# One-hots built token by token as contiguous rows, with a third of the neighbouring weight splits on GpSimd

## The chip, the cores and the metric

The kernel runs on one core of a Trainium2 chip. The metric is the device time of one execution in microseconds (us). TensorE (PE) multiplies matrices, VectorE (DVE) and ScalarE (ACT) work elementwise, GpSimd (POOL) is a fourth elementwise engine, and SyncE (SP) starts most of the transfers between memory and the on-chip SBUF. Each engine works through its own instructions in order; semaphores order the engines against each other. Matmul results land in PSUM.

## The reference

Two transformer blocks in float32 over one sequence of 256 tokens, width 1024. The second one ends with a layer of product-key experts (PEER), and the change lies there. Cut to what matters:

```python
def block(xb):                                   # 128 tokens at a time
    q = (xb @ w_query).reshape(128, 8, 2, 128)
    s = jnp.einsum('thpc,pkc->thpk', q, sub_keys)
    s1, i1 = lax.top_k(s[:, :, 0], 16)
    s2, i2 = lax.top_k(s[:, :, 1], 16)
    cand = (s1[..., :, None] + s2[..., None, :]).reshape(128, 8, 256)
    sc, ci = lax.top_k(cand, 16)
    e = take(i1, ci // 16) * 128 + take(i2, ci % 16)     # which of 16384 experts
    g = jax.nn.softmax(sc, axis=-1)
    act = jax.nn.gelu(jnp.einsum('td,thkd->thk', xb, expert_u[e]))
    return jnp.einsum('thk,thkd->td', g * act, expert_v[e])
```

Each token chooses 8 x 16 = 128 of 16384 experts, with a weight g for each.

## The kernel before

The kernel gathers nothing. It multiplies all tokens with all of expert_u and expert_v and makes the choice by a weight that is zero for every expert that was not chosen. All weights of both blocks stream through SBUF as 421 units of 128 x 1024 float32 numbers: `load` (SP) fetches unit u into one of four raw slots, `split` on ScalarE writes its rounded high half whi (three slots), `split` on VectorE writes the low half wlo = raw - whi (three slots), and TensorE multiplies in three products, high with high, high with low, low with high. The units named in the table LO_POOL get their low half from GpSimd (`split` in pool_program, L2074) with a semaphore of its own, lo_pool; TensorE's `whole(u)` and SP's `load` wait for the one or the other.

Units EU to EU + 127 are expert_u: `cols` (L456) makes 24 matmuls of 256 columns for each, eight blocks times three products, and ScalarE's `take_u` puts gelu of the result through stage into memory. In the first half VectorE finds the chosen experts and their weights beside this (`route`, L1904). At unit TURN_AT = 65 these are turned so that a token is a column: i1T and i2T hold the first and second key index of the 128 choices of each of the 256 tokens, g_hi and g_lo its weight in two fp16 parts. From unit HOT_FROM = 66 on, `hot_groups` spreads 64 groups of four tokens over the remaining units. For group g:

- VectorE (`one_hots`, L1990) builds three fp16 tables for the four tokens in X's place, called room: the one-hot of the first key, and the one-hot of the second key times g_hi and times g_lo. It compares keys, which holds 0 to 127, with the indices, one whole group in an instruction; the token is the innermost axis of room. Two groups fit, so group g waits until group g - 2 was multiplied (weighed).
- TensorE (L916) multiplies, for each token, the one-hot of the first key with both others: two matmuls of 128 columns into a 128 x 128 table of weights, eight matmuls a group, after the matmuls of its unit.
- ScalarE (`take_weights`, L1331) copies the tables of a group out of PSUM.

VectorE's program for unit n is: the groups of n, then the low half of unit n + 2. ScalarE's is: the tables of unit n - 1, the high half of unit n + 2 (which needs unit n - 1 used up), gelu of unit n - 1.

Units EV to EV + 127 are expert_v: `accumulate` (L930) adds twelve matmuls of 512 columns per unit to four PSUM banks, (t, d) being the half of the tokens and of the width. The last three units are written apart from the loop (L946 to L955), so that the bank of t = 0, d = 0 is finished first, and the closing norm starts with it. The order of all work is written out by hand.

Of the kernel before, what the change touches and what calls it, by code (L numbers as in the profile page):

```python
# [9 lines left out]
F16 = mybir.dt.float16  # L10
I32 = mybir.dt.int32
U32 = mybir.dt.uint32
ALU = mybir.AluOpType
# [36 lines left out]
UNITS = 421  # L50
V_ORDER = [*range(120, 128), *range(120)]

LO_POOL = (BR_B + 1, BR_B + 2, BR_B + 3, OUT, OUT + 1, UP, UP + 1, IN2, IN2 + 1, QUERY, EV + 1)

EXP_AT, TURN_AT, HOT_FROM = 42, 65, 66

# [25 lines left out]
def build(nc, A, out):  # L82
    with ExitStack() as ctx:

        def sb(stack, name, shape, dt=F32):
            return stack.enter_context(nc.sbuf_tensor(name, shape, dt))

        def signal(name, events, step=1):
            return Signal(ctx.enter_context(nc.semaphore(f"s_{name}")), events, step)
# [45 lines left out]
        def cs(name):  # L135
            return cst[:, CST[name][0]:CST[name][1]]
# [110 lines left out]
        i2T = sb(p4, "i2T", [128, 256], F16)  # L247
        g_hi = sb(p4, "g_hi", [128, 256], F16)
        g_lo = sb(p4, "g_lo", [128, 256], F16)
        keys = sb(p4, "keys", [128, 128, 4], F16)  # L250
        stage = sb(p4, "stage", [128, 8, 256])
        room = X[:, :, :].rearrange("p t n -> p (t n)").bitcast(F16)[:, 0:3072].rearrange("p (s w k t) -> p s w k t", s=2, w=3, t=4)
        gb4, squares, fin = raw[:, 0, :], raw[:, 1, :], raw[:, 2:4, :]


# [164 lines left out]
        ln_d = signal("ln_d", ["mean", "vc", "v", "r", "gain0", "gain1", "vn", "mixed0", "mixed1", "gated1"])  # L420
        fold_d = signal("fold_d", ["00", "10", "01", "11"])
        last_d = signal("last_d", ["00", "10", "01", "11"])
        routed = signal("routed", range(1, 99))
        route_d = signal("route_d", ["ex", "done", "turned1", "turned2"])
        query_d = signal("query_d", [1, 3, 5, 7, 9, 11, 13, 15])
        score_d = signal("score_d", range(4))
        hot_key = signal("hot_key", range(64))
        hot = signal("hot", range(64))
        taken_v = signal("taken_v", range(128))
        cut_d = signal("cut_d", range(128))  # L430
# [5 lines left out]
        def tensor_program(e):  # L436
# [451 lines left out]
            for n in range(128):  # L888
                if n == 1:
                    score(3)  # L890
                whole(EU + n)
                b = 4 + n % 4
                if n in (0, 1):
                    e.wait_ge(*(score_a if n % 2 == 0 else score_d).at(2))
                elif n in (2, 3):
                    e.wait_ge(*(score_a if n % 2 == 0 else score_d).at(3))
                elif n >= 4:
                    e.wait_ge(*gelu_u.at(n - 4))
                m = cols(EU + n, 0, 8, TH, TL, ps[b][:, 0:256], range(4))
                if n == 127:  # L900
                    m.then_inc(*half_used("u"))
                cols(EU + n, 0, 8, TH, TL, ps[b][:, 0:256], range(4, 8)).then_inc(*used(EU + n))
                for g in hot_groups(n):
                    e.wait_ge(*hot.at(g))
                    if g < 4:
                        if g == 0:
                            e.wait_ge(*route_a.at("turned0"))
                        if g == 1:
                            e.wait_ge(*route_d.at("turned1"))
                        if g == 2:  # L910
                            e.wait_ge(*route_d.at("turned2"))
                    else:
                        e.wait_ge(*weight_a.at(g - 4))
                    for i in range(4):
                        for w in (1, 2):
                            m = e.matmul(ps[g % 4][:, i * 128:i * 128 + 128], room[:, g % 2, 0, :, i], room[:, g % 2, w, :, i],  # L916
                                         start=w == 1, stop=w == 2)
                    m.then_inc(*weighed(g))
                if n == TURN_AT:
                    e.wait_ge(*route_d.at("done"))  # L920
                    e.wait_ge(*query_d.at(15))
                    e.wait_ge(*query_a.at(14))
                    for i, src in enumerate((ii[0], ii[1], gg)):
                        for t in range(2):
                            m = e.transpose(ps[i][:, t * 128:t * 128 + 128], src[:, t * 128:t * 128 + 128], ident)
                        m.then_inc(*turned(f"route{i}"))
# [10 lines left out]
            for n in range(125):  # L937
# [5 lines left out]
                    for d in range(2):  # L943
                        m = accumulate(n, t, d)
                m.then_inc(*used(EV + n))
            for n in range(125, 128):  # L946
                whole(EV + n)
                e.wait_ge(*cut_d.at(n))
            for n, d in ((125, 0), (125, 1), (126, 0), (126, 1)):
                accumulate(n, 0, d)  # L950
            for t in range(2):
                for d in range(2):
                    for n in range(125 if t else 127, 128):
# [435 lines left out]
        def vector_program(e):  # L1389
# [483 lines left out]

            e.tensor_copy(keys[:, :, :], bc(cs("iota"), 2, 4))

            def best16(n, vals, idx, src):

# [108 lines left out]


            def one_hots(g):  # L1990
                s, ts = g % 2, slice(4 * g, 4 * g + 4)
                h1, h2, h2_low = (room[:, s, w, :, :] for w in range(3))
                if g >= 2:
                    e.wait_ge(*weighed.at(g - 2))
                e.tensor_tensor(h2_low, keys[:, :, :], bc(i2T[:, ts], 1, 128), ALU.is_equal).then_inc(*hot_key(g))
                e.tensor_tensor(h1, keys[:, :, :], bc(i1T[:, ts], 1, 128), ALU.is_equal)
                e.wait_ge(*hot_key.at(g))
                e.tensor_tensor(h2, h2_low, bc(g_hi[:, ts], 1, 128), ALU.mult)
                e.tensor_tensor(h2_low, h2_low, bc(g_lo[:, ts], 1, 128), ALU.mult).then_inc(*hot(g))  # L1999

            def take(i):
                v = V_ORDER[i]
# [13 lines left out]
            for n in range(128):  # L2016
                if n < 64:
                    pull(UB1)
                for g in hot_groups(n):
                    if g == 0:  # L2020
                        e.wait_ge(*route_a.at("g_hi"))
                        e.wait_ge(*route_d.at("turned2"))
                        e.wait_ge(*d_kept.at(0))
                    one_hots(g)
                if n == 1:
                    score(3)
                split(EU + n + 2)
                if n == 127:
                    take(0)
                    for i in range(3):  # L2030
                        take(i + 1)
                        cut(i)
                if n == TURN_AT:
                    e.wait_ge(*turned.at("route1"))
                    e.tensor_copy(i2T[:, :], ps[1][:, 0:256]).then_inc(*route_d("turned1"))
                    e.wait_ge(*turned.at("route2"))
                    e.wait_ge(*route_a.at("g_hi"))
                    e.scalar_tensor_tensor(out=g_lo[:, :], in0=ps[2][:, 0:256], scalar=G_SCALE, in1=g_hi[:, :],
                                           op0=ALU.mult, op1=ALU.subtract).then_inc(*route_d("turned2"))
# [32 lines left out]
        def pool_program(e):  # L2072
# [23 lines left out]
            split(QUERY)  # L2096
            e.wait_ge(*low.at("x4.7"))
            e.dma_start(sub[:, :, :], A["sub_keys_2"]).then_inc(*d_sub(0))
            split(EV + 1)
            e.wait_ge(*lo.at(UNITS - 1))  # L2100
            e.dma_start(gb4, A["final_norm_g_2"].partition_broadcast(128)).then_inc(*d_gb4(0))
# [170 lines left out]
```

## Time and profile before

| | |
|---|---|
| median of 3 runs | 1370.74 us (1369.51 to 1370.87) |
| profiled execution: time, span | 1368.58 us, 1366.8 us |
| TensorE matmuls, weight loads (share of the span) | 96%, 88% |
| VectorE, ScalarE, GpSimd | 69%, 51%, 2% |
| granted TensorE clock, mean | 0.991 |

The profile shows one execution; the busy shares are means over stages with different limits, so a stage has to be read by itself. Matmuls overlap each other, and the start of one to the start of the next is what one costs.

### The profile page before, as it was taken

To read this page: it belongs to the slowest core of one execution; us is meant where nothing else is said; L and a number is where in the kernel's file an instruction comes from. 1 tells how busy PE (TensorE), PEld (TensorE's weight loads), DVE (VectorE), ACT (ScalarE), POOL (GpSimd) and SP (SyncE) were. 2 spreads that over 40 slices of the span, in tenths; PEclk is the share of its full clock that TensorE was granted. 3 is DMA by queue.
4 is the path that set the end of the run, shared out by engine and by line. 5 is a ranking of instruction groups with operands and counts; after the bars stand their busy time and mean duration, and the time that the engine had idled before them with its cause. 6 is when DMAs were issued, how large, how long until landed. Compare 5 with 4: busy or idle time off the path is not lost.

```text
span 1366.8 us, 22018 instructions
## 1 busy us (share of the span) xinstructions
PE 1316.4 (96%) x8592; PEld 1200.9 (88%) x8592; DVE 943.5 (69%) x1792; ACT 690.4 (51%) x1135; POOL 33.1 (2%) x27
## 2 busy tenths in 40 slices
PE   7999998999989899999999999999999999999996
PEld 6889978998877678999999999999988888888885
DVE  5765676674456755999899666676667676767665
ACT  5566456664455744444454444444444545454553
POOL 0000130000020000000000000000000000000000
PEclk9999999999999998999999999999999999999999
DMA  7533455666646335477767655555567676766763
GB/s 241 165 122 111 141 171 155 184 184 187 194 147 195 126 102 174 145 237 228 228 218 237 190 169 170 185 171 157 169 225 264 234 245 234 248 249 239 244 235 106
DMA packets 72662, 260.55 MB, mean 191 GB/s; under 512 B 8224, under 2 KB 8864, under 8 KB 72304
## 3 DMA queue, kind: packets, MB, share of 16 engines
q1 hardware_dynamic: 71520, 255.77, 57.7%
q0 software_dynamic: 1040, 3.38, 0.8%
q8 instruction: 69, 1.13, 0.3%
q14 instruction: 33, 0.27, 0.1%
HBM read 240.25 MB, written 18.87 MB: 190 GB/s over the span
## 4 chain that ended last, share of the span: by engine, by line
PE 87%; DVE 5%; ACT 4%; DMA 2%; issue 1%; SPq 0%; DVEq 0%; ACTq 0%
PE ps L933 24%; PE ps L453 14%; PE ps L461 13%; PE ps L462 13%; PE ps L463 13%; PE ps L916 4%; ACT whi L968 1%; PE ps L496 1%; DVE wlo L1396 1%; DVE mg L1654 1%; DMA raw<-in_expert_v_dram 1%; PE ps L471 1%; DMA raw<-in_w_in_dram 1%; PE ps L477 1%; DMA X<-in_x_dram 1%
## 5 line engine op out<-in xcount | busy, mean ns | idle before, releaser
L1396 DVE TENSOR_TENSOR wlo<-raw,whi 128x1024 fp32r<-128x1024 f32 (+2 forms) x410 | 498.0, 1216 | 352.8 <-ACT whi L968 350.7
L968 ACT ACTIVATE whi<-raw 128x1024 fp32r<-128x1024 f32 (+2 forms) x421 | 441.5, 1050 | 443.6 <-PE ps L463 166.0
L461 PE MATMUL ps<-TH,whi 128*128 128x256 f32 x1536 | 443.3, 289 | 2.3 <-DVE TL L1405 1.2
L462 PE MATMUL ps<-TL,whi 128*128 128x256 f32 x1536 | 436.3, 284 | 0.0
L463 PE MATMUL ps<-TH,wlo 128*128 128x256 f32 x1536 | 435.8, 284 | 0.0
L461 PEld LDWEIGHTS ps<-TH,whi 128*128 128x128 f32 x1536 | 296.9, 193 | 3.2 <-issue 3.0
L462 PEld LDWEIGHTS ps<-TL,whi 128*128 128x128 f32 x1536 | 296.3, 193 | 0.0
L463 PEld LDWEIGHTS ps<-TH,wlo 128*128 128x128 f32 x1536 | 295.7, 193 | 0.0
L933 PE MATMUL ps<-whi,TH 128*128 128x512 f32 x512 | 199.5, 390 | 5.2 <-DVE wlo L1396 3.7
L933 PE MATMUL ps<-whi,TL 128*128 128x512 f32 x512 | 199.2, 389 | 0.0
L933 PE MATMUL ps<-wlo,TH 128*128 128x512 f32 x512 | 199.2, 389 | 0.0
L933 PEld LDWEIGHTS ps<-whi,TH 128*128 128x128 f32 x512 | 96.1, 188 | 26.1 <-DVE wlo L1396 4.5
L933 PEld LDWEIGHTS ps<-whi,TL 128*128 128x128 f32 x512 | 96.1, 188 | 20.1
L933 PEld LDWEIGHTS ps<-wlo,TH 128*128 128x128 f32 x512 | 96.1, 188 | 19.7
L1334 ACT ACTIVATE ACTV<-ps 128x512 f32<-128x512 f32 x64 | 38.3, 598 | 123.9 <-PE ps L916 123.9
L453 PE MATMUL ps<-whi,TH 128*128 128x512 f32 (+1 forms) x208 | 79.1, 393 | 6.5 <-DVE wlo L1396 2.7
L453 PE MATMUL ps<-wlo,TH 128*128 128x512 f32 (+1 forms) x208 | 77.1, 383 | 0.0
L453 PE MATMUL ps<-whi,TL 128*128 128x512 f32 (+1 forms) x208 | 77.0, 383 | 0.0
L916 PE MATMUL ps<-X 128*128 128x128 f16 x512 | 70.7, 296 | 0.1
L2013 DVE TENSOR_TENSOR TL<-ACTV,TH 128x256 fp32r<-128x256 f32 x128 | 55.6, 434 | 0.5 <-ACT TH L974 0.5
L916 PEld LDWEIGHTS ps<-X 128*128 128x128 f16 x512 | 52.2, 118 | 3.6 <-DVE X L1999 0.3
L2009 DVE TENSOR_TENSOR ACTV<-ACTV,stage 128x256 f32<-128x256 f32 x128 | 53.6, 420 | 1.7 <-ACT ACTV L1334 1.7
(292 smaller groups left out, 1365.3 us busy)
## 6 DMA issues: line engine op xcount, KB each, us to landing
raw<-in_expert_u_dram SPq DMA_DIRECT2D x128, 512.0 KB, 3.7
raw<-in_expert_v_dram SPq DMA_DIRECT2D x128, 512.0 KB, 3.6
raw<-in_w_up_dram SPq DMA_DIRECT2D x32, 512.0 KB, 3.7
raw<-in_w_down_dram SPq DMA_DIRECT2D x32, 512.0 KB, 4.3
acts<-stage SPq DMA_DIRECT2D x32, 512.0 KB, 4.1
stage<-acts SPq DMA_DIRECT2D x30, 512.0 KB, 3.3
raw<-in_w_in_dram SPq DMA_DIRECT2D x20, 512.0 KB, 4.3
raw<-in_w_gate_dram SPq DMA_DIRECT2D x16, 512.0 KB, 3.5
```

The source lines that it names most:

```text
L453: m = e.matmul(o, x[:, k0 + j, sl], w[:, h, c:c + step], start=first, stop=last)
L461: e.matmul(dst, whi[:, h, sl], xh[:, k, :], start=k == 0, stop=False)
L462: e.matmul(dst, whi[:, h, sl], xl[:, k, :], start=False, stop=False)
L463: m = e.matmul(dst, wlo[:, h, sl], xh[:, k, :], start=False, stop=k == kn - 1)
L471: m = e.transpose(ps[b][:, at + t * 128:at + t * 128 + 128], src[:, t, c * 128:c * 128 + 128], ident)
L916: m = e.matmul(ps[g % 4][:, i * 128:i * 128 + 128], room[:, g % 2, 0, :, i], room[:, g % 2, w, :, i], start=w == 1, stop=w == 2)
L933: m = e.matmul(ps[bank4(t, d)][:, :], x[:, n % 8, sl], w[:, h, d * 512:d * 512 + 512], start=n == 0 and k == 0, stop=n == 127 and k == 2)
L968: e.activation(whi[:, u % NH, 0:n], raw[:, u % NR, 0:n], ACT.Copy).then_inc(*hi(u))
L1334: e.activation(ACTV[:, :, 4 * g:4 * g + 4], ps[g % 4][:, :].rearrange("p (t k) -> p k t", t=4), ACT.Copy, scale=1.0 / G_SCALE).then_inc(*w ...
L1396: e.tensor_tensor(wlo[:, u % NH, 0:n], raw[:, u % NR, 0:n], whi[:, u % NH, 0:n].bitcast(F32), ALU.subtract).then_inc(*lo(u))
L2009: e.tensor_tensor(ACTV[:, v, :], ACTV[:, v, :], stage[:, v % 8, :], ALU.mult).then_inc(*taken_v(i))
L2013: e.tensor_tensor(TL[:, i % 8, :], ACTV[:, V_ORDER[i], :], TH[:, i % 8, :].bitcast(F32), ALU.subtract).then_inc(*cut_d(i))
```

## The change

It has three parts. First, `one_hots` works through the four tokens of a group one by one: three tensor_scalar instructions for each, over 128 contiguous numbers, that take the token's index and weight as per-partition scalars from i1T, i2T, g_hi and g_lo; comparing and multiplying are one instruction. room is laid out with the token outside and the key innermost, keys loses its copy for four tokens, the wait between the two old steps (hot_key) is gone, and the first group waits for keys. Second, LO_POOL gets 20 more units, EU + 67 to EU + 124 in steps of three, so GpSimd makes their low halves and VectorE does not. Third, of the last three units each is waited for where its matmuls stand, instead of all three ahead of the first.

```diff
-LO_POOL = (BR_B + 1, BR_B + 2, BR_B + 3, OUT, OUT + 1, UP, UP + 1, IN2, IN2 + 1, QUERY, EV + 1)
+LO_POOL = (BR_B + 1, BR_B + 2, BR_B + 3, OUT, OUT + 1, UP, UP + 1, IN2, IN2 + 1, QUERY,
+           *range(EU + 67, EU + 127, 3), EV + 1)
...
-        keys = sb(p4, "keys", [128, 128, 4], F16)
+        keys = sb(p4, "keys", [128, 128], F16)
...
-        room = X[:, :, :].rearrange("p t n -> p (t n)").bitcast(F16)[:, 0:3072].rearrange("p (s w k t) -> p s w k t", s=2, w=3, t=4)
+        room = X[:, :, :].rearrange("p t n -> p (t n)").bitcast(F16)[:, 0:3072].rearrange("p (s w t k) -> p s w t k", s=2, w=3, t=4)
...
-                            m = e.matmul(ps[g % 4][:, i * 128:i * 128 + 128], room[:, g % 2, 0, :, i], room[:, g % 2, w, :, i],
+                            m = e.matmul(ps[g % 4][:, i * 128:i * 128 + 128], room[:, g % 2, 0, i, :], room[:, g % 2, w, i, :],
                                          start=w == 1, stop=w == 2)
...
-            for n in range(125, 128):
+            for n in range(125, 127):
                 whole(EV + n)
                 e.wait_ge(*cut_d.at(n))
-            for n, d in ((125, 0), (125, 1), (126, 0), (126, 1)):
-                accumulate(n, 0, d)
+                for d in range(2):
+                    accumulate(n, 0, d)
+            whole(EV + 127)
+            e.wait_ge(*cut_d.at(127))
...
-            e.tensor_copy(keys[:, :, :], bc(cs("iota"), 2, 4))
+            e.tensor_copy(keys[:, :], cs("iota")).then_inc(*route_d("keys"))
...
             def one_hots(g):
-                s, ts = g % 2, slice(4 * g, 4 * g + 4)
-                h1, h2, h2_low = (room[:, s, w, :, :] for w in range(3))
+
                 if g >= 2:
                     e.wait_ge(*weighed.at(g - 2))
-                e.tensor_tensor(h2_low, keys[:, :, :], bc(i2T[:, ts], 1, 128), ALU.is_equal).then_inc(*hot_key(g))
-                e.tensor_tensor(h1, keys[:, :, :], bc(i1T[:, ts], 1, 128), ALU.is_equal)
-                e.wait_ge(*hot_key.at(g))
-                e.tensor_tensor(h2, h2_low, bc(g_hi[:, ts], 1, 128), ALU.mult)
-                e.tensor_tensor(h2_low, h2_low, bc(g_lo[:, ts], 1, 128), ALU.mult).then_inc(*hot(g))
+                for i in range(4):
+                    first, second, second_low = (room[:, g % 2, w, i, :] for w in range(3))
+                    at = slice(4 * g + i, 4 * g + i + 1)
+                    e.tensor_scalar(first, keys[:, :], i1T[:, at], None, ALU.is_equal)
+                    e.tensor_scalar(second, keys[:, :], i2T[:, at], g_hi[:, at], ALU.is_equal, ALU.mult)
+                    m = e.tensor_scalar(second_low, keys[:, :], i2T[:, at], g_lo[:, at], ALU.is_equal, ALU.mult)
+                m.then_inc(*hot(g))
...
+            for u in range(EU + 67, EU + 127, 3):
+                split(u)
             split(EV + 1)
```

VectorE's instructions at unit 66, the first with one-hots; X is room's place. Before:

```order
641 L2038 SCALAR_TENSOR_TENSOR g_lo<-ps,g_hi 128x256
642 L1995 TENSOR_TENSOR X<-keys,i2T 128x512
643 L1996 TENSOR_TENSOR X<-keys,i1T 128x512
644 L1998 TENSOR_TENSOR X<-X,g_hi 128x512
645 L1999 TENSOR_TENSOR X<-X,g_lo 128x512
```

The change, at the same place:

```order
641 L2042 SCALAR_TENSOR_TENSOR g_lo<-ps,g_hi 128x256
642 L1999 TENSOR_SCALAR X<-keys,i1T 128x128
643 L2000 TENSOR_SCALAR X<-keys,i2T,g_hi 128x128
644 L2001 TENSOR_SCALAR X<-keys,i2T,g_lo 128x128
645 L1999 TENSOR_SCALAR X<-keys,i1T 128x128
```

Four instructions for a group become twelve, each a quarter as wide; they read only keys and columns of the index and weight tables, never what one of them wrote.

TensorE's last three units, from unit 125's last matmul of its first half on; ps0 to ps3 are the four banks. In both kernels unit 125's own wait stands six matmuls ahead. Before:

```order
7785 L933 MATMUL ps1<-whi,TL 128x512
7786 L933 MATMUL ps0<-whi,TH 128x512
7787 L933 MATMUL ps0<-wlo,TH 128x512
...
7791 L933 MATMUL ps1<-whi,TL 128x512
7792 L933 MATMUL ps0<-whi,TH 128x512
```

The change:

```order
7785 L933 MATMUL ps1<-whi,TL 128x512
7786 L933 MATMUL ps0<-whi,TH 128x512 [waits s_cut_d,s_lo]
7787 L933 MATMUL ps0<-wlo,TH 128x512
...
7791 L933 MATMUL ps1<-whi,TL 128x512
7792 L933 MATMUL ps0<-whi,TH 128x512 [waits s_cut_d,s_lo]
```

The matmuls stand in the same order (the rows 7788 to 7790 between are left out); before, the first matmul of unit 125 carries the waits of all three units, now the first of 126 (7786) and of 127 (7792) have their own.

## Rows read from the trace of the kernel before

**Rows 1.** the page, chain that ended last: shares by engine.

```profile
PE 87%; DVE 5%; ACT 4%; DMA 2%; issue 1%; SPq 0%; DVEq 0%; ACTq 0%
```

**Rows 2.** stretch: us, busy us (instructions) of PE, PEld, DVE, ACT, POOL; clock; DMA.

```profile
768.26:1001.89 233.63, 233.57 (x1956) 229.93 (x1955) 159.01 (x313) 110.84 (x183) 0.00 (x0) 1.00 0.54 170
```

**Rows 3.** chain in order of time, one unit of the stage: start us, us, what.

```profile
881.33 0.12 PE ps L463
881.45 0.95 PE ps L916 x8
```

**Rows 4.** timeline of DVE, two units: start us, us, instruction, [idle before].

```profile
884.01 1.23 DVE L1396 TENSOR_TENSOR wlo<-raw,whi 128x1024 fp32r<-128x1024 f32 x1 [1.25 <-ACT whi L968]
885.16 0.42 DVE L1995 TENSOR_TENSOR X<-keys,i2T 128x512 f16<-128x512 f16 x1
...
887.84 1.23 DVE L1396 TENSOR_TENSOR wlo<-raw,whi 128x1024 fp32r<-128x1024 f32 x1 [1.26 <-ACT whi L968]
```

**Rows 5.** timeline of DVE at the first one-hots.

```profile
766.60 0.43 DVE L1995 TENSOR_TENSOR X<-keys,i2T 128x512 f16<-128x512 f16 x1
...
767.94 0.42 DVE L1995 TENSOR_TENSOR X<-keys,i2T 128x512 f16<-128x512 f16 x1
```

**Rows 6.** chain in order of time, expert_v units.

```profile
1021.18 326.73 PE ps L933 x1440
```

**Rows 7.** weight loads by shape: xcount, busy us, mean ns, idle before.

```profile
L916 PEld LDWEIGHTS ps<-X 128*128 128x128 f16 x512 | 52.2, 118 | 3.6 <-DVE X L1999 0.3
...
L477 PEld LDWEIGHTS ps<-cst,qk 128*128 128x128 f32 x16 | 1.8, 141 | 0.1
...
L477 PEld LDWEIGHTS ps<-cst,kcat 128*96 128x96 f32 x16 | 1.8, 126 | 0.0
```

**Rows 8.** DVE instructions by shape: xcount, busy us, mean ns.

```profile
L1400 DVE TENSOR_SCALAR xn<-X,st 128x512 f32<-128x512 f32 x2 | 0.9, 482 | 0.0
```

**Rows 9.** timeline of DVE, three stretches.

```profile
26.42 0.35 DVE L1400 TENSOR_SCALAR mg<-cst,st 128x128 f32<-128x128 f32 x2
26.69 1.22 DVE L1396 TENSOR_TENSOR wlo<-raw,whi 128x1024 fp32r<-128x1024 f32 x1
...
513.84 0.88 DVE L1400 TENSOR_SCALAR xn<-X,st 128x512 f32<-128x512 f32 x2
...
696.51 0.29 DVE L1930 TENSOR_SCALAR ACTV<-ACTV 128x256 uint32<-128x256 uint32 x1
696.71 0.29 DVE L1931 TENSOR_SCALAR ACTV<-ACTV 128x256 uint32<-128x256 uint32 x1
```

**Rows 10.** timeline of POOL and DVE, two stretches.

```profile
167.04 2.39 POOL L2077 TENSOR_TENSOR wlo<-raw,whi 128x1024 fp32r<-128x1024 f32 x1 [164.04 <-ACT whi L968]
...
168.56 0.42 DVE L1627 SCALAR_TENSOR_TENSOR sg<-sg,ps 128x256 f32<-128x256 f32 x1 [0.94 <-PE ps L463]
...
178.07 2.38 POOL L2077 TENSOR_TENSOR wlo<-raw,whi 128x1024 fp32r<-128x1024 f32 x1 [1.76 <-ACT whi L968]
...
178.41 2.31 DVE L1654 TENSOR_TENSOR mg<-sg,mg 128x256 f32<-128x256 f32 x1
```

**Rows 11.** chain in order of time, the end.

```profile
1343.81 4.09 PE ps L933 x18
...
1347.99 1.06 ACT whi L968
...
1349.08 1.24 DVE wlo L1396
...
1350.55 3.66 PE ps L933 x15
...
1357.91 1.41 DVE raw L2067 x2
```

**Rows 12.** DMA issues: queue, count, KB each, median us to landing.

```profile
raw<-in_expert_u_dram SPq DMA_DIRECT2D x128, 512.0 KB, 3.7
...
raw<-in_final_norm_g_dram POOLq DMA_DIRECT2D x1, 512.0 KB, 4.2
```

More of the change, by code:

```diff
@@ L422, in build @@
         last_d = signal("last_d", ["00", "10", "01", "11"])
+        route_d = signal("route_d", ["keys", "ex", "done", "turned1", "turned2"])
         routed = signal("routed", range(1, 99))
-        route_d = signal("route_d", ["ex", "done", "turned1", "turned2"])
         query_d = signal("query_d", [1, 3, 5, 7, 9, 11, 13, 15])
         score_d = signal("score_d", range(4))
-        hot_key = signal("hot_key", range(64))
         hot = signal("hot", range(64))
@@ L2022, in vector_program @@
                         e.wait_ge(*route_d.at("turned2"))
+                        e.wait_ge(*route_d.at("keys"))
                         e.wait_ge(*d_kept.at(0))
```

## The prediction, made before the result was known

> **What bounds the kernel now.** I read the chain that ended last first: TensorE holds 87% of it [rows 1]. Then I split the time by stage. In the stage of the change (the second half of the expert_u units, 768.26 to 1001.89) TensorE is busy for 233.57 of 233.63 us at granted clock 1.00 (2.4 GHz), VectorE for 159 [rows 2]. So the stage lasts as long as TensorE's stream: a unit's 24 matmuls of 256 columns follow each other every 0.12 us, and a group's eight one-hot matmuls take 0.95 us, 0.119 each, although they have only 128 columns [rows 3]. The reader should see that half the columns cost the same. VectorE waits for ScalarE before every low half: low half at 884.01, one-hots from 885.16, next low half at 887.84 [rows 4]. Of a unit of 3.83 us it needs 1.15 for the low half and 1.34 for four one-hot instructions (766.60 to 767.94) [rows 5]; 1.33 are spare.
>
> **TensorE's term.** The 512-column stream takes 326.73 us for 1440, 0.227 each [rows 6]; that is 0.107 more than for 256, 0.418 ns a column, with 13 ns fixed. At this rate 128 columns would take 0.0666 us; measured are 0.119. Is it the weight load? A load that is 128 wide takes 141 ns, one 96 wide 126 [rows 7]: 0.47 ns a column, so some 81 ns are fixed, and the fp16 load of 118 ns holds about 37 ns of loading, which is not 119. What is left is that both operands are read at every fourth element (the token is innermost). With contiguous rows I take 0.0666, 0.53 us a group; if the 37 ns of loading don't overlap with the matmul it is 0.104, 0.83 a group; from above, no change at 0.945. I choose the low end because every other stream of the trace hides its loads.
> The Trainium skill, "Advanced Engine Details and Errata", section "Memory Cachelines", speaks against this part: SBUF needs two hits on a 16-byte line for full speed, and a stride of four fp16 elements has two. By it the layout costs nothing and the term is nil; the measured 0.119 for 128 columns does not fit it well.
>
> **VectorE's term.** A group becomes 12 tensor_scalars of 128 fp16 elements in place of four tensor_tensors of 512: 768 in all instead of 256. The trace has no fp16 tensor_scalar and none with two scalars read from SBUF. First the rates. A low half (1024 fp32 elements) occupies 1.15 us, a one-hot tensor_tensor (512 fp16) 0.335 [rows 4, 5]; with two fp16 elements a cycle, 1024a + f = 1.15 and 256a + f = 0.335 give a cycle of 1.06 ns and a fixed part of 0.06. Two tensor_scalars of 512 fp32 elements with one scalar from SBUF take 0.88 with 0.48 for one [rows 8, 9], so the next starts after 0.40: two elements a cycle, 0.27, and 0.13 fixed. Without such a scalar 256 elements start 0.20 apart [rows 9]: 0.135 and 0.065. So one scalar costs 0.066. For fp16 I take four elements a cycle (twice fp32's two, as with tensor_tensor): 0.034 + 0.134 = 0.168. Bounds: one pair with a scalar took 26.42 to 26.69, 0.135 each for 128 fp32 elements [rows 9], so no price for the scalar and 0.100; if a second scalar costs 0.066 again, 0.234 on the 512 two-scalar instructions. I take 0.168 for all: the longer pair shows the scalar's price plainly, and no row says that a second read waits for the first. A group is then 2.02 us, 129.0 in all (before 85.8).
>
> **GpSimd's part.** 20 low halves leave VectorE; of the 61 of the stage 41 stay, 41 x 1.15 = 47.2. GpSimd takes 2.39 for one [rows 10]. What it does to VectorE is the open point. A tensor_tensor with two SBUF inputs at 178.41 took 2.31 us, where its like takes 0.42: it stood until GpSimd's instruction from 178.07 was over. One with a PSUM input ran in 0.42 beside another (168.56, in 167.04 to 169.43) [rows 10]. The new tensor_scalars read one SBUF tensor, but at twice the rate of the instruction that stood, so I take them as nearer to the blocked one: 2.25 us lost for each of 20 (2.39 less the front that runs on), 45.0. From below: nothing.
> The Trainium skill, "SBUF — State Buffer", section "Who interferes with whom", says that a tensor_scalar in a two-port mode and a GpSimd instruction exclude each other for a whole instruction. The rows show it for a tensor_tensor only; by this rule the sum is the one that I take.
>
> **The sum of the stage.** VectorE starts its first one-hot at 766.60 [rows 5] and then has 129.0 + 47.2 + 45.0 = 221.2 us in a row up to the last one-hots, 987.8; TensorE's last group ends some 0.6 later, at 988.4 against 1001.9: 13.5 us saved. TensorE alone would be done earlier: group 1 can't end before 771.3, then 60 units of 2.878 and 62 groups of 0.53 make 977. So VectorE, not TensorE, would set the stage; behind TensorE's wait for hot stand the next unit's matmuls, and ScalarE waits for these.
> GpSimd's low halves are not late: the high half is there at about 884.0, GpSimd would be done at 886.4, and TensorE uses it two units on, near 889. Behind its 20 waits stand only the low half of EV + 1 and gb4, both due later. SP's loads behind lo_pool come some 1.2 us later; a slot refilled then is read four units after, some 9 us, and a landing takes 3.7 [rows 12]: covered. The smaller keys cast and the dropped wait on hot_key are at most 0.3 us, once or beside a full VectorE, and I take them as nothing.
>
> **The end.** Now TensorE waits at unit 125 for all of the last three units: its work ends about 1347.7 (the last result is there at 1347.90), ScalarE's last high half starts at 1347.99, the low half at 1349.08, and the 15 matmuls up to the first finished bank take 3.66 from 1350.55 [rows 11]. With a wait at each unit the 12 first-half matmuls of units 125 and 126 (2.72 us) run in that gap of 2.8, and the first bank is done 2.7 earlier. The chain behind it alternates between VectorE and ScalarE and moves with it. What is late next is gb4: issued when the last low half is through, about 1350.5, 4.2 to land [rows 12], 1354.7, needed at 1357.91 - 2.7 = 1355.2; were these 0.5 us of cover gone, the rest would be lost again. 2.7 saved.
>
> Together 16.2: 1368.58 - 16.2 = 1352.4 for the profiled execution. The median of the runs shown is 2.16 above it, so I forecast 1354.5.
>
> **Rivals.**
> 1. GpSimd does not block tensor_scalars, or the scalar read is cheap (0.135 an instruction takes 25 off VectorE's 221): TensorE sets the stage, 977 against 1001.9, 24.9 + 2.7 saved, 1343.1. With loading that doesn't overlap (62 x 0.30 = 18.6 more) 1361.7. For it: the row at 168.56 and the pair at 26.42; against: the one at 178.41.
> 2. Slower: the second scalar costs another 0.066 on 512 instructions, 33.8 us, all on VectorE, which is the bound: 33.8 - 16.2 = 17.6 slower, 1388.3. It decides from 16.2/512 = 32 ns on. For it: the first scalar's 0.066 looks like a latency, which may be paid anew; against: nothing but that two reads can overlap.
> 3. The layout does nothing for TensorE: 0.945 a group remain, VectorE's 988 is below that, and only the end is saved, less 1.0 for the later start: 1369.0. For it: the trace has no fp16 matmul on contiguous rows; against: nothing else explains 0.119.
>
> **Chances.** Forecast 0.40 (1349 to 1361 by itself: some 10 ns on 768 instructions, and the load that may not overlap), rival 1 0.27, rival 2 0.21, rival 3 0.12. Times of this kernel can be told apart by about 0.2%, 2.7 us. The forecast and rival 1 are faster, 0.67; rival 3 is the same, 0.12; rival 2 slower, 0.21. The range goes from 1340, just under rival 1, to 1384, which takes in the forecast, rivals 1 and 3 and a second scalar of up to some 55 ns.
>
> **What would show it.** One-hot matmuls every 0.067 us (right), 0.104 or 0.119 (rival 3). One-hot instructions 0.17 apart and one of 2.3 us beside each GpSimd instruction; if none is stretched, rival 1; if there are two kinds, 0.17 and 0.23, rival 2. TensorE's idle time in the stage with VectorE's one-hots as releaser: some 11 us in the forecast, near 1 in rival 1, over 40 in rival 2. At the end no wait of 2.7 us before unit 125. I am wrong too if the many short VectorE instructions hold GpSimd up, so that TensorE waits for lo_pool.

## The result, and the profile of the changed kernel

The change made the kernel slower: 1378.22 us median against 1370.18 in the same sitting, ratio 1.0076 with a 95% interval of 1.0058 to 1.0094, so 8 to 13 us lost. The ratios of this document are the record's estimates from the fast runs of both kernels, not quotients of the two medians (here 1.0059). The forecast was 1354.5. The profiled execution has a span of 1376.7 us, 9.9 more than before.

The chain that ended last, shares by engine, first line of that part of the page (TensorE had 87% in [rows 1]):

```profile
PE 73%; DVE 20%; ACT 4%; issue 1%; DMA 1%; SPq 0%; DVEq 0%; ACTq 0%
```

VectorE took 20% of the chain, almost all of it in the stage of the one-hots. The same stretch as in [rows 2], same columns:

```profile
768.26:1001.89 233.63, 202.33 (x1826) 196.29 (x1824) 229.13 (x751) 104.25 (x173) 45.17 (x19) 0.96 0.49 159
```

TensorE, which had no gap here before, now waits for 31 us, and VectorE is full: 229.13 of 233.63 us where it was 159. The granted clock averages 0.96 in place of 1.00, which is between the two levels of 1.2 and 2.4 GHz (0.50 and 1.00). It was at the lower one in four stretches, each of which began behind or inside a wait of TensorE for one-hots; the longest, with the same columns:

```profile
852.84:859.66 6.82, 6.02 (x32) 5.97 (x32) 6.55 (x29) 1.82 (x3) 0.00 (x0) 0.50 0.28 81
```

TensorE had been idle for 1.44 us just ahead of it and was idle for 1.82 us across its start; in it the matmuls of 256 columns start 0.21 us apart in place of 0.12. The waits inside the stage, by engine and releaser (us in total, times, longest), for TensorE and then for VectorE:

```profile
PE ps L916 <- DVE X L2001: 32.0, 22, 2.1
...
DVE wlo L1398 <- ACT whi L970: 4.4, 4, 2.0
```

So TensorE waits for nothing but one-hots (L2001 is the last of a group), and VectorE itself hardly waits. The longest of its four waits for ScalarE stands right behind the stretch at the lower clock:

```profile
861.93 1.22 DVE L1398 TENSOR_TENSOR wlo<-raw,whi 128x1024 fp32r<-128x1024 f32 x1 [1.97 <-ACT whi L970]
```

The next two (1.16 and 0.97 us) follow two of the other such stretches in the same way, within 4 us. ScalarE's high half waits until TensorE has used up a unit, so a slower TensorE would explain these waits; no run tests it. Where VectorE's time goes is seen in its timeline, and in GpSimd's beside it (start, us):

```profile
873.70 1.23 DVE L1398 TENSOR_TENSOR wlo<-raw,whi 128x1024 fp32r<-128x1024 f32 x1
874.84 0.26 DVE L1999 TENSOR_SCALAR X<-keys,i1T 128x128 f16<-128x128 f16 x1
875.00 0.32 DVE L2000 TENSOR_SCALAR X<-keys,i2T,g_hi 128x128 f16<-128x128 f16 x1
875.23 0.32 DVE L2001 TENSOR_SCALAR X<-keys,i2T,g_lo 128x128 f16<-128x128 f16 x1
875.45 0.26 DVE L1999 TENSOR_SCALAR X<-keys,i1T 128x128 f16<-128x128 f16 x1
...
876.83 2.47 DVE L2000 TENSOR_SCALAR X<-keys,i2T,g_hi 128x128 f16<-128x128 f16 x1
879.21 0.30 DVE L2001 TENSOR_SCALAR X<-keys,i2T,g_lo 128x128 f16<-128x128 f16 x1
...
876.88 2.37 POOL L2081 TENSOR_TENSOR wlo<-raw,whi 128x1024 fp32r<-128x1024 f32 x1 [9.14 <-ACT whi L970]
```

Two things are to be read there, from the starts, not from the durations. The one-scalar instruction costs 0.16 (874.84 to 875.00), each two-scalar one 0.22 to 0.23 (875.00, 875.23, 875.45). And an instruction that should take 0.22 holds VectorE for 2.38 us (876.83 to 879.21), exactly while GpSimd's low half runs: 2.16 us lost, where a low half on VectorE itself takes 1.14 (873.70 to 874.84). There are 19 such rows in the stage, one for each GpSimd low half in it; the twentieth ran at 761.89, ahead of the first one-hot. The instructions' own spread over the stage (ns min/median/max, first to last start in us) says the same:

```profile
L1999 DVE TENSOR_SCALAR X<-keys,i1T x256: 235/245/264, 765.2 to 1013.1; 128x128 f16<-128x128 f16 x128
L2000 DVE TENSOR_SCALAR X<-keys,i2T,g_hi x256: 296/306/2472, 765.4 to 1013.2; 128x128 f16<-128x128 f16 x128
L2001 DVE TENSOR_SCALAR X<-keys,i2T,g_lo x256: 296/305/2496, 765.6 to 1013.4; 128x128 f16<-128x128 f16 x128
```

The chain in order of time shows TensorE's side and the end:

```profile
1004.19 0.46 PE ps L916 x8
...
1014.33 0.48 PE ps L916 x8
...
1033.99 330.14 PE ps L933 x1455
1364.15 0.70 DVE X L2060
```

A group's eight one-hot matmuls take 0.46 us where they took 0.95 [rows 3]: that part of the change does what it should. But the last group ends at 1014.8 in place of 1001.9 [rows 2], 12.9 late. At the end TensorE runs from its first expert_v units to the closing norm without a gap: 330.14 us from 1033.99 on, where the first bank was done 333.03 us after the start of these units (1021.18 in [rows 6] to 1350.55 + 3.66 in [rows 11]). That gives 2.9 back, and 12.9 - 2.9 = 10.0 is the 9.9 of the spans.

### The profile page after: what moved, and what is told of

Same layout as the page of the kernel before. It is cut to its first block, busy times and chain, and to the rows that moved or that the text cites. A ratio compares the mean times of both kernels' runs of the same rounds, so it can differ in the third digit from the quotient of the medians.

```text
span 1376.7 us, 22531 instructions
## 1 busy us (share of the span) xinstructions
PE 1297.9 (94%) x8592; PEld 1179.7 (86%) x8592; DVE 1026.5 (75%) x2284; ACT 690.8 (50%) x1135; POOL 80.7 (6%) x47
## 4 chain that ended last, share of the span: by engine, by line
PE 73%; DVE 20%; ACT 4%; issue 1%; DMA 1%; SPq 0%; DVEq 0%; ACTq 0%
PE ps L933 24%; PE ps L453 15%; PE ps L461 10%; PE ps L462 10%; PE ps L463 10%; DVE X L2000 6%; DVE X L2001 4%; DVE wlo L1398 4%; DVE X L1999 3%; ACT whi L970 1%; PE ps L496 1%; PE ps L471 1%; DVE mg L1656 1%; DMA X<-in_x_dram 1%; DMA raw<-in_expert_v_dram 1%
## 5 line engine op out<-in xcount | busy, mean ns | idle before, releaser
L1398 DVE TENSOR_TENSOR wlo<-raw,whi 128x1024 fp32r<-128x1024 f32 (+2 forms) x390 | 473.1, 1215 | 282.9 <-ACT whi L970 280.8
L2081 POOL TENSOR_TENSOR wlo<-raw,whi 128x1024 fp32r<-128x1024 f32 x31 | 73.8, 2382 | 913.1 <-ACT whi L970 913.1
L2000 DVE TENSOR_SCALAR X<-keys,i2T,g_hi 128x128 f16<-128x128 f16 x256 | 112.6, 440 | 0.0
L2001 DVE TENSOR_SCALAR X<-keys,i2T,g_lo 128x128 f16<-128x128 f16 x256 | 84.8, 331 | 0.0
L916 PE MATMUL ps<-X 128*128 128x128 f16 x512 | 40.4, 223 | 32.1 <-DVE X L2001 32.0
```

What stands on the lines that cost most here:

```text
L1398: e.tensor_tensor(wlo[:, u % NH, 0:n], raw[:, u % NR, 0:n], whi[:, u % NH, 0:n].bitcast(F32), ALU.subtract).then_inc(*lo(u))
L2000: e.tensor_scalar(second, keys[:, :], i2T[:, at], g_hi[:, at], ALU.is_equal, ALU.mult)
L2001: m = e.tensor_scalar(second_low, keys[:, :], i2T[:, at], g_lo[:, at], ALU.is_equal, ALU.mult)
L2081: e.tensor_tensor(wlo[:, u % NH, 0:n], raw[:, u % NR, 0:n], whi[:, u % NH, 0:n].bitcast(F32), ALU.subtract).then_inc(*lo_pool(u))
```

## The experiments

Each is compared by the ratio to the kernel before in its own sitting (a sitting is a set of runs taken together; medians of before there: 1366.9, 1369.1 and 1368.3), so that a time on the scale of 1370.2 is ratio x 1370.2. Runs 3, 7, 8 and 9 are single executions without a ratio; they are read for what their traces show.

**1. Without GpSimd's 20 units.**

```diff
-           *range(EU + 67, EU + 127, 3), EV + 1)
+           EV + 1)
...
-            for u in range(EU + 67, EU + 127, 3):
-                split(u)
```

> The changed kernel without the 20 units on GpSimd: VectorE makes their low halves again; one-hots, layout and the last units' waits stay as changed. Theory (each GpSimd low half stands VectorE still for about 2.2 us and saves it only 1.14): VectorE then needs 64 x 2.436 us for the groups and 61 x 1.14 for the low halves from 765.2 on, 225.5 in all, so the stage ends near 991 in place of 1014.9, and the kernel takes about 1355 (1351 to 1359). Rival (the long VectorE rows beside GpSimd cost nothing on balance, VectorE is merely full of short instructions): 20 x 1.14 = 23 us more work for the engine that sets the stage, about 1401. Second rival (something other than VectorE sets the stage): 1378, no change.

Measured: 1353.37 us, ratio 0.9889 (0.9869 to 0.9910), 1355.0 on the scale: what the first theory said. VectorE made 20 more low halves and the kernel became faster than the changed one, by 25 us by the ratios (0.9889 against 1.0076) and by 23 by the two traces (spans of 1353.4 and 1376.7 us). The last group ends at 991.6, where the theory had 991. Its stage, same columns as above, shows VectorE full still, with useful work now:

```profile
766.50:980.00 213.50, 205.99 (x1863) 196.23 (x1861) 213.43 (x789) 105.91 (x176) 0.00 (x0) 0.98 0.55 176
```

**2. The second scalar as a constant.** The weights are left out of the output here.

```diff
-                    e.tensor_scalar(second, keys[:, :], i2T[:, at], g_hi[:, at], ALU.is_equal, ALU.mult)
+                    e.tensor_scalar(second, keys[:, :], i2T[:, at], 1.0, ALU.is_equal, ALU.mult)
```

and the same for second_low.

> The changed kernel with the second scalar of its 512 two-scalar instructions replaced by the constant 1.0: the weights g_hi and g_lo are left out, so the output lacks them; operations, layout and GpSimd stay. Theory (the second scalar that is read from SBUF costs 0.060 us by itself): one-hot instructions all start 0.163 apart, VectorE needs 768 x 0.163 + 41 x 1.14 + 20 x 2.2 = 216 us, and the time is about 1347.5 (1343 to 1352). Rival (the 0.060 belongs to the second operation, not to where its operand lies): the spacing stays 0.223 and the time 1378.

Measured: 1347.52, ratio 0.9859 (0.9837 to 0.9882), 1350.9 on the scale. VectorE's timeline:

```profile
879.91 0.25 DVE L2001 TENSOR_SCALAR X<-keys,i2T 128x128 f16<-128x128 f16 x1
880.07 0.25 DVE L1999 TENSOR_SCALAR X<-keys,i1T 128x128 f16<-128x128 f16 x1
880.23 0.25 DVE L2000 TENSOR_SCALAR X<-keys,i2T 128x128 f16<-128x128 f16 x1
880.39 2.40 DVE L2001 TENSOR_SCALAR X<-keys,i2T 128x128 f16<-128x128 f16 x1
882.71 0.24 DVE L1999 TENSOR_SCALAR X<-keys,i1T 128x128 f16<-128x128 f16 x1
```

All are 0.16 apart, with two operations still: the price is that of reading a scalar, not of the operation. The stretched row beside GpSimd stays. With this one price taken away the kernel is 3.6 us from the forecast of 1354.5.

**3. No, one and two scalars in one kernel.** The first index and g_hi are left out.

```diff
-                    e.tensor_scalar(first, keys[:, :], i1T[:, at], None, ALU.is_equal)
-                    e.tensor_scalar(second, keys[:, :], i2T[:, at], g_hi[:, at], ALU.is_equal, ALU.mult)
+                    e.tensor_scalar(first, keys[:, :], 5.0, None, ALU.is_equal)
+                    e.tensor_scalar(second, keys[:, :], i2T[:, at], 1.0, ALU.is_equal, ALU.mult)
```

> The changed kernel with a constant in place of the first one-hot's index and of the second's weight, so that its three instructions read no, one and two scalars from SBUF; the first index and g_hi are left out. Theory (each scalar costs 0.060): the three start 0.103, 0.163 and 0.223 apart. Rival (the first scalar is free, only the second costs): 0.163, 0.163, 0.223. By the first the time is about 1345, by the second about 1360.

Measured: 1349.08 in one execution. VectorE's timeline:

```profile
875.63 0.18 DVE L1999 TENSOR_SCALAR X<-keys 128x128 f16<-128x128 f16 x1
875.73 0.24 DVE L2000 TENSOR_SCALAR X<-keys,i2T 128x128 f16<-128x128 f16 x1
875.89 0.30 DVE L2001 TENSOR_SCALAR X<-keys,i2T,g_lo 128x128 f16<-128x128 f16 x1
876.12 0.18 DVE L1999 TENSOR_SCALAR X<-keys 128x128 f16<-128x128 f16 x1
```

0.10, 0.16 and 0.23 to the next start: each scalar costs some 0.06 us, the first one too. The time, 1349.08 in one execution, is 4 above the 1345 that the theory gave; the spacings decide between the theories. At 128 elements two scalars cost more than the rest of the instruction.

**4. The last units' waits alone, on the kernel before.**

```diff
-            for n in range(125, 128):
+            for n in range(125, 127):
                 whole(EV + n)
                 e.wait_ge(*cut_d.at(n))
-            for n, d in ((125, 0), (125, 1), (126, 0), (126, 1)):
-                accumulate(n, 0, d)
+                for d in range(2):
+                    accumulate(n, 0, d)
+            whole(EV + 127)
+            e.wait_ge(*cut_d.at(127))
```

> The kernel before with the last units' waits alone changed. Theory: the first bank is done 2.7 to 2.9 us earlier and all behind it moves along, so 1367.4 (1366.5 to 1368.3). Rival (the transfer of the last norm's weights is late next): at most 0.5 us are saved, 1369.7.

Measured: 1363.77, ratio 0.9972 (0.9958 to 0.9986), 3.8 us faster with 1.9 and 5.8 as bounds. The chain:

```profile
1019.41 330.14 PE ps L933 x1455
```

The same 330.14 as in the changed kernel, 2.9 less than before, and no wait for the norm's weights behind it; so the theory held, and the rival's 0.5 us lie below the interval. The start of these units at 1019.41 in place of 1021.18 [rows 6] lies ahead of the edit and is scatter.

**5. GpSimd's 20 units alone, on the kernel before.** The edit is the two lines of the first experiment, the other way round.

> The kernel before with the 20 units on GpSimd alone changed: four one-hot instructions of 512 elements a group in the old layout. Theory (VectorE stands still some 2.2 us in every third unit, but has 1.33 spare in a unit and is relieved of 1.14, and TensorE sets the stage): no change, 1370 (1369 to 1372). Rival (the group whose instruction stands comes late for TensorE, the slack of a unit cannot be carried over to the next): up to 1 us in each of 20 units, up to 1390.

Measured: 1366.74, ratio 1.0000 (0.9984 to 1.0015). VectorE's timeline, and GpSimd's:

```profile
878.36 0.42 DVE L2000 TENSOR_TENSOR X<-X,g_lo 128x512 f16<-128x512 f16 x1
882.52 1.23 DVE L1397 TENSOR_TENSOR wlo<-raw,whi 128x1024 fp32r<-128x1024 f32 x1 [3.75 <-ACT whi L969]
...
878.73 2.39 POOL L2078 TENSOR_TENSOR wlo<-raw,whi 128x1024 fp32r<-128x1024 f32 x1 [9.08 <-ACT whi L969]
```

No change, and by a better reason than the theory's: VectorE had finished its groups, and GpSimd's 2.39 us lay in an idle time of 3.75. With the others it was the same: no one-hot instruction of the stage took longer than 0.47. So this run says nothing on whether these tensor_tensors would stand; it says that GpSimd's help is harmless where VectorE idles, and was not needed there.

**6. The layout alone, with whole-group instructions.** Contiguous rows, but four tensor_tensors of 512 a group, no GpSimd units.

```diff
-                e.tensor_tensor(h2_low, keys[:, :, :], bc(i2T[:, ts], 1, 128), ALU.is_equal).then_inc(*hot_key(g))
+                e.tensor_tensor(h2_low, bc(keys[:, :], 1, 4), bc(i2T[:, ts], 2, 128), ALU.is_equal).then_inc(*hot_key(g))
```

(against the kernel before; the other three likewise.)

> Contiguous rows and the last units' waits as changed, no low halves on GpSimd, and the one-hots built by the kernel before's four tensor_tensors of 512 elements a group, with the index and weight repeated along the 128 keys. Theory (the gain of the layout is TensorE's, and the two scalars were the price of the token by token form): the instructions stay 0.335 apart, VectorE needs 2.48 of a unit's 3.34 us, TensorE sets the stage, which ends near 972 against 1001.9 before; about 1338 on the scale of the kernel before's 1370.2 (ratio 0.974 to 0.980). Rival (an operand that is repeated along its innermost axis is read at one element a cycle): the instructions are 0.60 apart, VectorE needs 224 us and sets the stage, about 1354, no better than the tensor_scalars.

Measured: 1352.16, ratio 0.9878 (0.9860 to 0.9897), 1353.5 on the scale: the theory fell, the rival's 0.60 is there in the timeline of VectorE.

```profile
876.37 0.68 DVE L1999 TENSOR_TENSOR X<-keys,i2T 128x512 f16<-128x512 f16 x1
876.97 0.68 DVE L2000 TENSOR_TENSOR X<-keys,i1T 128x512 f16<-128x512 f16 x1
877.57 0.68 DVE L2002 TENSOR_TENSOR X<-X,g_hi 128x512 f16<-128x512 f16 x1
```

The token by token form (2.44 us a group) and this one (2.41) cost VectorE the same, so there was nothing to win by it. The 0.335 were had only in the old layout, where the index and the weight of the four tokens lie side by side innermost; here each is repeated there.

**7 and 8. Which operand's stride costs TensorE the time.** One of them is put back to every fourth element. The view spread names the same place with the token innermost; the matmul reads it likewise.

```diff
-                    e.tensor_scalar(first, keys[:, :], i1T[:, at], None, ALU.is_equal)
+                    e.tensor_scalar(spread[:, g % 2, 0, i, :], keys[:, :], i1T[:, at], None, ALU.is_equal)
```

for the stationary operand, and second and second_low in the same way for the moving ones.

> The changed kernel without the 20 units on GpSimd, and with only the first one-hot (TensorE's stationary operand) written and read with the token innermost again, every fourth element. Theory A (the stationary operand's stride costs TensorE the time): the one-hot matmuls are 0.118 apart again. Theory B (the moving operand's stride does): they stay at 0.057. Whatever VectorE pays for writing every fourth element shows in the spacing of the first instruction, 0.163 where it costs nothing.

> The changed kernel without the 20 units on GpSimd, and with only the two weighted one-hots (TensorE's moving operands) written and read with the token innermost again. Theory A (the stationary operand's stride costs TensorE the time): the one-hot matmuls stay 0.057 apart. Theory B (the moving operand's does): 0.118, and TensorE needs 3.82 us of a unit again, so that about 1367 is the least that the kernel can take.

Measured, one execution each: 1362.92 and 1371.72. Eight one-hot matmuls in TensorE's timeline, from the first start to the last end, and the duration of one (ns min/median/max), first with the stationary operand strided:

```profile
873.55 0.64 PE L917 MATMUL ps<-X 128*128 128x128 f16 x8
```

```profile
L917 PE MATMUL ps<-X x512: 219/219/250, 768.3 to 998.9; 128*128 128x128 f16 x171
```

and with the moving ones:

```profile
876.06 1.09 PE L917 MATMUL ps<-X 128*128 128x128 f16 x8
```

```profile
L917 PE MATMUL ps<-X x512: 273/294/296, 766.8 to 1007.0; 128*128 128x128 f16 x171
```

(0.64 - 0.22) / 7 = 0.060 apart with the stationary operand strided, (1.09 - 0.29) / 7 = 0.114 with the moving ones. Theory B: the moving operand's stride was nearly the whole cost for TensorE. VectorE's timeline in the first of the two runs shows what writing at this stride costs:

```profile
875.18 0.38 DVE L2000 TENSOR_SCALAR X<-keys,i1T 128x128 f16<-128x128 f16 x1
875.38 0.32 DVE L2001 TENSOR_SCALAR X<-keys,i2T,g_hi 128x128 f16<-128x128 f16 x1
```

The strided one-hot is 0.20 from the next start (0.196 in the median of 256), the contiguous one 0.163.

**9. Which VectorE instructions stand beside GpSimd.**

```diff
-                    e.tensor_scalar(first, keys[:, :], i1T[:, at], None, ALU.is_equal)
-                    e.tensor_scalar(second, keys[:, :], i2T[:, at], g_hi[:, at], ALU.is_equal, ALU.mult)
-                    m = e.tensor_scalar(second_low, keys[:, :], i2T[:, at], g_lo[:, at], ALU.is_equal, ALU.mult)
+                    for w, (index, weight) in enumerate(((i1T, g_hi), (i2T, g_hi), (i2T, g_lo))):
+                        m = e.scalar_tensor_tensor(out=room[:, g % 2, w, i, :], in0=keys[:, :], scalar=index[:, at],
+                                                   in1=weight[:, at].broadcast_to([128, 128]), op0=ALU.is_equal, op1=ALU.mult)
```

> The changed kernel with all 768 one-hot instructions as scalar_tensor_tensor: the index stays a scalar, the weight comes as a second tensor operand (one column repeated 128 times); the first one-hot takes g_hi too, which it has no use for, so the output's weights are off. GpSimd's 20 units stay. It asks which VectorE instructions stand beside GpSimd. Theory (only an instruction that runs at more than one element a cycle stands, and this form doesn't): none of the 768 is stretched to 2 us. Rival (any instruction that takes all its operands from SBUF stands): one of 2.3 us beside each GpSimd instruction. Spacing, an estimate from 1.06 ns a cycle and 0.06 for the start and for the scalar: 0.26; the stage then ends near 1012 by the theory (about 1376) and near 1056 by the rival (about 1419).

Measured: 1417.82 in one execution. The timeline of GpSimd and of VectorE beside it, and TensorE's waits:

```profile
878.11 8.45 POOL L2080 TENSOR_TENSOR wlo<-raw,whi 128x1024 fp32r<-128x1024 f32 x1 [5.37 <-ACT whi L970]
...
883.14 1.21 DVE L1398 TENSOR_TENSOR wlo<-raw,whi 128x1024 fp32r<-128x1024 f32 x1
884.28 2.44 DVE L1999 SCALAR_TENSOR_TENSOR X<-keys,i1T,g_hi 128x128 f16<-128x128 f16 x1
886.64 0.34 DVE L1999 SCALAR_TENSOR_TENSOR X<-keys,i2T,g_hi 128x128 f16<-128x128 f16 x1
```

```profile
PE ps L461 <- POOL wlo L2080: 40.2, 19, 2.5
```

The theory fell: this slower form (0.26 apart, as estimated) stands too, one row for each GpSimd low half, and the time is the rival's. But GpSimd stood as well: its instruction was open from 878.11 to 886.56, while VectorE's 0.26 us instructions went on undisturbed until its own low half (883.14); right behind that one, VectorE stood from 884.28 to 886.64, the 2.4 us that GpSimd takes alone [rows 10]. So TensorE now waits for GpSimd's low halves too.

**10. The first one-hot of a whole group in the old layout.** Only the moving operands have to be contiguous (7 and 8), so the stationary one can be built by one cheap instruction. keys4 is keys repeated for four tokens, as in the kernel before. No GpSimd units.

```diff
-                    e.tensor_scalar(first, keys[:, :], i1T[:, at], None, ALU.is_equal)
+                e.tensor_tensor(spread, keys4[:, :, :], bc(i1T[:, ts], 1, 128), ALU.is_equal)
```

> No low halves on GpSimd; the last units' waits as changed; the first one-hot (TensorE's stationary operand) of a whole group made by one tensor_tensor with the token innermost as in the kernel before, the two weighted ones (the moving operands) token by token in contiguous rows as changed. Theory: one-hot matmuls stay 0.057 apart, VectorE needs 64 x (0.335 + 8 x 0.223) + 69.5 = 205 us from 765 on, which ends at 971 like TensorE's own 972, so about 1338 on the scale of the kernel before's 1370.2 (ratio 0.974 to 0.981). Rival (two engines that are both full trip over each other, and each wait is lost): 5 to 10 us more, 1345.

Measured: 1339.72, ratio 0.9806 (0.9787 to 0.9825), 1343.6 on the scale. The ratio lies at the upper edge of the theory's range and does not exclude the rival's 1345; the trace is the theory's. Its execution took 1337.35 us, the last group ends at 973.7 where 972 was expected, and both engines are almost full:

```profile
768.26:970.00 201.74, 201.08 (x1896) 198.23 (x1895) 199.73 (x609) 107.68 (x178) 0.00 (x0) 1.00 0.59 194
```

In the stage TensorE waits for one-hots for 0.7 us in all, where the rival had 5 to 10.

**11. The weights on the first one-hot.**

```diff
+                e.tensor_tensor(first_low, keys4[:, :, :], bc(i1T[:, ts], 1, 128), ALU.is_equal).then_inc(*hot_key(g))
+                for i in range(4):
+                    e.tensor_scalar(room[:, g % 2, 0, i, :], keys[:, :], i2T[:, 4 * g + i:4 * g + i + 1], None, ALU.is_equal)
+                e.wait_ge(*hot_key.at(g))
+                e.tensor_tensor(first, first_low, bc(g_hi[:, ts], 1, 128), ALU.mult)
+                e.tensor_tensor(first_low, first_low, bc(g_lo[:, ts], 1, 128), ALU.mult).then_inc(*hot(g))
```

in place of the twelve tensor_scalars; the matmul's stationary operand is spread[w], its moving one room[0].

> As the run with the first one-hot of a whole group, but the weights go to the first one-hot: one comparison and two multiplications of a whole group with the token innermost (stationary operands), and four one-scalar tensor_scalars for the second one-hot, contiguous (the moving operand of both matmuls). The products are the same. Theory: VectorE needs 64 x (3 x 0.335 + 4 x 0.163) + 69.5 = 175.5 us, TensorE sets the stage at 2.88 + 0.46 us a unit and ends near 972: 1338 (ratio 0.973 to 0.979), and VectorE waits for ScalarE again before each low half. Rival (something that was hidden sets the unit, such as ScalarE's high half, which needs the unit before used up and then the low half): 3.5 us a unit, about 1347.

Measured: 1340.01, ratio 0.9799 (0.9783 to 0.9814), 1342.7 on the scale: 2.0% faster than before, 2.8% faster than the change, and no different from run 10. The stretch of the stage, a row of VectorE's timeline, and two of the chain:

```profile
768.26:970.00 201.74, 201.74 (x1905) 199.20 (x1903) 173.93 (x488) 108.28 (x179) 0.00 (x0) 1.00 0.61 194
```

```profile
876.18 1.23 DVE L1401 TENSOR_TENSOR wlo<-raw,whi 128x1024 fp32r<-128x1024 f32 x1 [0.53 <-ACT whi L973]
```

```profile
966.51 0.48 PE ps L919 x8
966.99 0.17 PE ps L464
...
969.92 0.48 PE ps L919 x8
```

TensorE is full again and VectorE waits 0.53 us before each low half, as the theory had it. A unit is 3.41 us (966.51 to 969.92) and not 3.34: the group takes 0.48, and the matmul behind it 0.17 instead of 0.12. Over 61 units those 0.07 are 4.3 us, of which the end of the stage shows 1.8 (973.8 for 972), because the first one-hot matmul starts at 766.2, some 2 us earlier than before. The profiled execution took 1338.51, the theory's 1338; what is left of the 4.7 us between the theory and the scale is not in this trace. The ratio lies just above the theory's 0.979 and below the rival's 1347 (0.983).

## Why the prediction was wrong

The time lay inside the range, but on the other side of no change. VectorE did set the stage, as forecast, and its sum can be checked term by term. Of the signs that the prediction named, the two kinds of one-hot instructions came (0.16 and 0.22 apart, rival 2), TensorE's idle time behind one-hots was 32 us (the forecast had 11, rival 2 over 40), and GpSimd was not held up (2.37 to 2.42 us a low half).

| VectorE in the stage, us | predicted | measured |
|---|---|---|
| one-hot instructions | 768 x 0.168 = 129.0 | 256 x 0.163 + 512 x 0.223 = 155.9 |
| low halves | 41 x 1.15 = 47.2 | 41 x 1.14 = 46.7 |
| stood beside GpSimd | 20 x 2.25 = 45.0 | 19 x 2.16 = 41.0 |
| waiting for ScalarE | 0 | 4.4 |
| sum | 221.2 | 248.0 |

The measured sum, from the first one-hot at 765.2 on, ends at 1013.2; the last instruction starts at 1013.4.

- **The step that failed** is the one in VectorE's term: "I take 0.168 for all: the longer pair shows the scalar's price plainly, and no row says that a second read waits for the first." Runs 2 and 3 show that the second one is paid in full: each scalar adds 0.06, and the second makes 0.223 of 0.163. That lifts the one-hots from 129.0 to 155.9, 26.9 us on an engine that had become the bound, more than the 16.2 of the whole forecast gain. It is rival 2, whose own limit was 32 ns a second scalar; 60 were paid. For the profiled execution the rival would have 1388.3 - 2.2 = 1386.1, and 1378.5 was measured, 7.6 less. Its sum for VectorE was 8.4 too high: 0.234 was taken where 0.223 is right (512 x 0.011 = 5.6), 20 blocked instructions of 2.25 for 19 of 2.16 (4.0), the one-scalar price and the low halves (1.8) and a start 1.4 earlier, less the 4.4 of waiting. The last group ended 1.6 and not 0.6 behind that sum, which takes 1.0 off, and the end gave 0.2 more.
- **The first scalar** was sized rightly from a pair of 512 elements in [rows 8, 9] (0.066). The sum made of it was a little off: the 0.13 fixed and 0.034 make 0.164 and not 0.168, and 0.163 was measured. The pair of 128 elements at 26.42, which I used as the lower bound, misled: in run 3 an instruction without a scalar costs 0.10, with one 0.16. Nor were its two instructions 0.135 each; [rows 9] shows them merged, and the second one by itself is

```profile
26.50 0.28 DVE L1400 TENSOR_SCALAR mg<-cst,st 128x128 f32<-128x128 f32 x1
```

so 0.08 to the second start and 0.19 from it to the low half at 26.69. The 0.19 is near what a full scalar price gives (0.065 + 0.068 for the elements + 0.066 = 0.20); why the first took only 0.08 stays open.
- **GpSimd blocks tensor_scalars**: right, and nearly to the size. Run 1 shows what the prediction had not said: taken by itself this part of the change loses. 2.16 us of VectorE are given for 1.14, once VectorE is the bound, and removing it is worth 23 to 25 us. The prediction charged the 45.0 but never set them against the 23 that they bought. The Trainium skill, "SBUF — State Buffer", section "Who interferes with whom", has the exclusion for a whole instruction; the 2.47 us rows agree.
- **TensorE's layout**: right, 0.46 a group for 0.53. The choice that the load is hidden held. The reason was half right: not both operands' stride cost the time, almost all of it was the moving operand's (runs 7 and 8). The Trainium skill's section "Memory Cachelines" in "Advanced Engine Details and Errata" would make a stride of four fp16 elements free; here it cost 0.114 against 0.060, and the measurement decides. VectorE's writes cost more at that stride as well (run 7).
- **The end**: right. 2.7 forecast, 2.9 in the trace, run 4 alone 3.8 (1.9 to 5.8). The norm's weights came in time.

What the two right terms are worth together is shown by runs 10 and 11: with the layout where it counts, no low halves on GpSimd and fewer scalars read, TensorE is the bound again, at 0.980 of the time before.

## What to carry to other kernels

A scalar read from SBUF had a fixed price per instruction here, 0.06 us each, so an edit that cuts instructions to a quarter of their width and adds scalars must be costed by their number: 512 second scalars outweighed a stage's gain. Work given to a helper engine has to be charged with what it blocks on the engine it relieves, in that stage: harmless where VectorE idled (run 5), a loss of 23 to 25 us where it was full (run 1). Before a layout is changed for two operands, change one: nearly all of the time was the moving one's, and the two fastest versions (runs 10 and 11) kept the other as it was.

## What was not expected of the hardware

- GpSimd and VectorE shut each other out for a whole instruction in the changed kernel and in run 9, but not the same one waited: between tensor_scalars GpSimd got in at once (2.37 us long, in the changed kernel), between scalar_tensor_tensors with two SBUF tensors it was kept out until VectorE's next low half was through, and was open for 7 to 10 us (run 9, 19 low halves). Why stays open.
- A tensor_tensor whose second operand repeats along its innermost axis ran at little more than half the rate, 0.60 for 0.335 us (run 6, as its rival had it).
